# One step of a two-layer hybrid decoder: p and gate weights fetched and split early, 1/rms by Ln and Exp, the beginning in another order

## What is computed

```python
for l in range(2):
    h = h + 0.5 * swiglu(rms_norm(h, g1[l]), wi1[l], wo1[l])      # ffn 2l
    h = h + mixer[l](rms_norm(h, gm[l]))                          # conv and mLSTM, or two attentions
    h = h + 0.5 * swiglu(rms_norm(h, g2[l]), wi2[l], wo2[l])      # ffn 2l+1
    h = h + sigmoid(rms_norm(h, gp[l]) @ wg[l]) * (p[l] @ wp[l])  # the gate phase, "ple"
y = rms_norm(h, g_final)

def rms_norm(x, g, eps=1e-6):
    return x * lax.rsqrt(jnp.mean(x * x, axis=-1, keepdims=True) + eps) * g
```

## Time and profile before

| | us |
|---|---|
| median of 3 runs | 2738.8 |
| lowest and highest | 2735.88 and 2739.21 |
| the profiled execution, as a run | 2746.85 |
| its span, from the first to the last instruction | 2745.0 |
| PE busy in it | 2599.5 |

### The profile page before, as it was taken

The page is one execution under the profiler, slowest core; times in us unless marked ns, Lnnn a source line. Parts: engine busy times, 40 slices in busy tenths (PEclk is TensorE's granted clock), DMA queues, the critical chain, the costliest instruction groups (busy, mean ns, idle before and its releaser), DMA issues. The chain is left out here.

```text
span 2745.0 us, 44639 instructions
## 1 busy us (share of the span) xinstructions
PE 2599.5 (95%) x18322; PEld 2456.3 (89%) x18322; DVE 927.2 (34%) x1558; ACT 767.5 (28%) x954; POOL 811.0 (30%) x206
## 2 busy tenths in 40 slices
PE   7999999898889999999999999999789799999997
PEld 6999999895579999999999999999455599999997
DVE  4211224686653211224321122311755432202234
ACT  4222223223223222224322222311444432212232
POOL 3333333221023333333333343432000033343332
PEclk9999999998789999999999999999876699999998
DMA  4222223310112222222222222234211022222122
GB/s 145 82 83 90 77 77 110 70 62 31 48 60 82 76 81 88 80 72 76 102 76 77 100 77 77 101 112 157 93 62 47 16 77 77 76 92 77 69 85 73
DMA packets 66902, 220.57 MB, mean 80 GB/s; under 512 B 14007, under 2 KB 31287, under 8 KB 51195
## 3 DMA queue, kind: packets, MB, share of 16 engines
q1 hardware_dynamic: 51280, 200.68, 21.2%
q10 hardware_dynamic: 15530, 18.63, 2.4%
HBM read 207.95 MB, written 11.33 MB: 80 GB/s over the span
## 5 line engine op out<-in xcount | busy, mean ns | idle before, releaser
L430 POOL TENSOR_TENSOR wl<-raw,wr 128x2048 fp32r<-128x2048 f32 (+2 forms) x200 | 807.3, 4036 | 1905.9 <-ACT wr L858 1905.9
L440 PE MATMUL ps<-xr,wr 128*128 128x256 f32 (+1 forms) x2432 | 727.3, 299 | 39.5 <-POOL wl L430 23.4
L442 PE MATMUL ps<-xr,wl 128*128 128x256 f32 (+1 forms) x2432 | 724.9, 298 | 0.0
L441 PE MATMUL ps<-xl,wr 128*128 128x256 f32 (+1 forms) x2432 | 724.9, 298 | 0.0
L440 PEld LDWEIGHTS ps<-xr,wr 128*128 128x128 f32 x2432 | 466.2, 192 | 43.5 <-issue 36.2
L440 PE MATMUL ps<-x2r,wr 128*128 128x256 f32 (+1 forms) x1664 | 491.8, 296 | 0.5 <-POOL wl L430 0.5
L442 PE MATMUL ps<-x2r,wl 128*128 128x256 f32 (+1 forms) x1664 | 490.0, 294 | 0.0
L441 PE MATMUL ps<-x2l,wr 128*128 128x256 f32 (+1 forms) x1664 | 489.9, 294 | 0.0
L441 PEld LDWEIGHTS ps<-xl,wr 128*128 128x128 f32 x2432 | 466.2, 192 | 0.2
L442 PEld LDWEIGHTS ps<-xr,wl 128*128 128x128 f32 x2432 | 465.7, 191 | 0.0
L858 ACT ACTIVATE wr<-raw 128x2048 fp32r<-128x2048 f32 (+1 forms) x200 | 351.6, 1758 | 369.6 <-PE ps L442 294.3
(11 more groups left out here) (312 smaller groups left out, 2027.8 us busy)
## 6 DMA issues: line engine op xcount, KB each, us to landing
raw<-in_up SPq DMA_DIRECT2D x88, 1024.0 KB, 4.8
raw<-in_down SPq DMA_DIRECT2D x32, 768.0 KB, 4.2
raw<-in_mixin SPq DMA_DIRECT2D x24, 1024.0 KB, 4.8
raw<-in_down SPq DMA_DIRECT2D x32, 640.0 KB, 3.9
raw<-in_ple SPq DMA_DIRECT2D x16, 640.0 KB, 3.9
raw<-in_mixout SPq DMA_DIRECT2D x8, 1024.0 KB, 4.9
kc<-in_kc SPq DMA_DIRECT2D x32, 256.0 KB, 3.5
vc<-in_vc SPq DMA_DIRECT2D x32, 256.0 KB, 3.5
```

Of the source, the lines that this page charges most:

```text
L430: e.tensor_tensor(wl[s][:, 0:p.width], raw[s][:, 0:p.width], wr[s][:, 0:p.width].bitcast(F32), ALU.subtract).then_inc(S(f"w_split{s}"), 1)
L440: e.matmul(out, wrt, xrt, start=first, stop=False)
L441: e.matmul(out, wrt, xlt, start=False, stop=False)
L442: return e.matmul(out, wlt, xrt, start=False, stop=last)
```

## The change

- **p.** `praw` moves to memory behind x2l, and its rounded part and residual take the last two blocks of `hr` and `hl`, which the second chunk of an ffn doesn't use. The load is issued ahead of ffn 1 and ffn 3; ACT rounds it and DVE makes its residual between "up" and "down" of the second chunk of these ffn.
- **Gate weights and history.** The gate weights are loaded at the beginning, and rounded and split in ffn 0, between "up" and "down" of the first chunk. The history is loaded from SP's queue once the last "down" tile of ffn 0 is done. ACT stores the fourth bias row in "glu" behind the first Sigmoid, and DVE waits for the stores in the first block of "glu", where it also sets the fringe of `vn`.
- **1/rms.** `root` makes Ln and then Exp of -0.5 times it on ACT, with the table set for both loaded ahead of its wait; the reciprocal on DVE goes.
- **The beginning.** POOL no longer sets `raw` to zero. The first weight load comes right behind the parameters on SP's queue, then four of the eight blocks of x (the odd ones), then, once block 4 has landed, the second weight load. ACT issues the even blocks, loads the table set ahead, and rounds the first weights behind the second block's square. Squares go to `sq` and `hd` in turn and are summed in two PSUM banks, the last sum into `acc`; the residual of the third block comes behind the first three sums. The first norm's `norm_sum` stands in the second tile's third step.

The diff, with the unchanged lines around it cut:

```diff
     x2l = sb("x2l", [P, KD, T], F32R, at=[X2_AT + KD * T * 4])
-    praw = sb("praw", [P, KP, T], at=z)
-    pr = sb("pr", [P, KP, T], F32R, at=z)
-    pl = sb("pl", [P, KP, T], F32R, at=z)
+    praw = sb("praw", [P, KP, T], at=[X2_AT + 2 * KD * T * 4])
+    assert CHUNKS[0] - CHUNKS[1] == KP
+    pr, pl = hr[:, CHUNKS[1]:, :], hl[:, CHUNKS[1]:, :]
     z = [ZONE]
...
         e.dma_start(prm[:], A["prm"]).then_inc(S("prm_loaded"), 16)
-        def load_pair(p, i):
+        def load_pair(p, i, first=False):
             for s in range(2):
+                if first and s == 1:
+                    for j in range(1, KD, 2):
+                        e.dma_start(h[:, j, :], A["xT"][:, j, :]).then_inc(S(f"h_loaded{j}"), 16)
+                    e.wait_ge(S(f"h_loaded{KD // 2}"), 16)
...
             p = ph[name]
+            if name in (order[0], "glu"):
+                load_pair(p, 0, first=name != "glu")
+            if name == "glu":
+                e.wait_ge(S("tile_done"), done_at(("down", 0, 1), KD - 1))
+                e.dma_start(us[:, :, :, 0:HIST], A["hist"]).then_inc(S("hist_loaded"), 16)
             if name != ("out", 1):
-                with e.Fori(0, p.nb // 2) as i:
+                with e.Fori(1 if name in (order[0], "glu") else 0, p.nb // 2) as i:
                     load_pair(p, i)
...
         for s in range(2):
-            e.memset(raw[s][:], 0.0).then_inc(S(f"w_split{s}"), 1)
+            e.nop().then_inc(S(f"w_split{s}"), 1)
         for name in order:
...
             p = ph[name]
+            norm_at = (0, 5) if norm else (1, 2)
...
                         for k in range(kn_):
-                            if first and t == 0 and k == 5:
+                            if first and (t, k) == norm_at:
                                 norm_sum(norm)
...
+            e.preload_act_table_set("natural_log_exp_and_others")
             e.wait_ge(S("ss_ready"), m + 1)
-            e.activation(two(R[:]), psn, ACT.Sqrt, scale=1.0 / D, bias=eps6[:, 0:1]).then_inc(S("root_ready"), 1)
+            e.activation(two(R[:]), psn, ACT.Ln, scale=1.0 / D, bias=eps6[:, 0:1]).then_inc(S("root_ready"), 1)
+            e.wait_ge(S("root_ready"), m + 1)
+            e.activation(R[:], R[:], ACT.Exp, scale=-0.5).then_inc(S("R_ready"), 1)
...
                     store_bias_row(2 * c)
+                    if c == 0:
+                        e.wait_ge(S("wg_loaded"), 16)
+                        e.activation(wgr[:], wgraw[:], ACT.Copy).then_inc(S("wgr_ready"), 1)
+                if n % 2 and c == 1:
+                    e.wait_ge(S("p_loaded"), 16 * (n // 2 + 1))
+                    e.activation(pr, praw[:], ACT.Copy).then_inc(S("pr_ready"), 1)
                 down_phase(n, c, m + 1 if c else None)
-                if n == 0:
-                    store_bias_row(2 * c + 1)
-
-
-        for j in range(KD):
+                if (n, c) == (0, 0):
+                    store_bias_row(1)
+
+
+        for j in range(0, KD, 2):
             e.dma_start(h[:, j, :], A["xT"][:, j, :]).then_inc(S(f"h_loaded{j}"), 16)
+        e.preload_act_table_set("natural_log_exp_and_others")
         e.wait_ge(S("prm_loaded"), 16)
...
             head(0, j, (S(f"h_loaded{j}"), 16))
-            square(0, j, None)
-            if j == KD // 2:
+            if j >= 2:
+                e.wait_ge(S("acc_done"), j - 1)
+            e.activation((sq, hd)[j % 2][:], h[:, j, :], ACT.Square).then_inc(S("sq_ready"), 1)
+            if j == 1:
                 round_block(order[0], 0, 0, first=True)
...
         e.dma_start(pages[:], A["pages"]).then_inc(S("pages_loaded"), 16)
+        e.dma_start(wgraw[:], A["wg"]).then_inc(S("wg_loaded"), 16)
         e.wait_ge(S("ones_ready"), 3)
...
-        e.dma_start(wgraw[:], A["wg"]).then_inc(S("wg_loaded"), 16)
-        e.dma_start(us[:, :, :, 0:HIST], A["hist"]).then_inc(S("hist_loaded"), 16)
-        e.wait_ge(S("wg_loaded"), 16)
-        e.activation(wgr[:], wgraw[:], ACT.Copy).then_inc(S("wgr_ready"), 1)
         for n in blocks("glu", 1):
...
             e.activation(sg[:], tu[:], ACT.Sigmoid).then_inc(S("glu_sig"), 1)
+            if n == 0:
+                store_bias_row(3)
...
         e.wait_ge(S("m_stored"), 16)
+        e.dma_start(praw[:], A["pT"][0]).then_inc(S("p_loaded"), 16)
         ffn(1, 2)
...
             m = 4 * l + 4
-            e.dma_start(praw[:], A["pT"][l]).then_inc(S("p_loaded"), 16)
             name = ("ple", l)
             for n in blocks(name, m - 1):
-                if n == 0:
-                    e.wait_ge(S("p_loaded"), 16 * (l + 1))
-                    e.activation(pr[:], praw[:], ACT.Copy).then_inc(S("pr_ready"), 1)
                 e.wait_ge(S("tile_evacuated"), evac_at(name, 2 * n))
...
         e.wait_ge(S("kv_stored"), 32)
+        e.dma_start(praw[:], A["pT"][1]).then_inc(S("p_loaded"), 16)
         ffn(3, 6)
...
         def factor(m):
-            e.wait_ge(S("root_ready"), m + 1)
-            e.reciprocal(R[:], R[:]).then_inc(S("R_ready"), 1)
             e.wait_ge(S("R_ready"), m + 1)
...
                     copy_bias_row(2 * c)
+                    if c == 0:
+                        e.wait_ge(S("wgr_ready"), 1)
+                        e.tensor_tensor(wgl[:], wgraw[:], wgr[:].bitcast(F32), ALU.subtract).then_inc(S("wg_split"), 2)
+                if n % 2 and c == 1:
+                    e.wait_ge(S("pr_ready"), n // 2 + 1)
+                    e.tensor_tensor(pl, praw[:], pr.bitcast(F32), ALU.subtract).then_inc(S("p_split"), 1)
                 if c:
...
+        acc_ps = ps[:, 6:8, 0:HALF]
         e.wait_ge(S("prm_loaded"), 16)
...
             e.wait_ge(S(f"h_loaded{j}"), 16)
-            rest(0, j)
-            add_square(0, j, j == 0)
+            if j != 2:
+                rest(0, j)
+            for q in {1: (0, 1, 2), 2: ()}.get(j, (j,) if j else ()):
+                e.wait_ge(S("sq_ready"), q + 1)
+                src = two((sq, hd)[q % 2][:])
+                if q == 0:
+                    e.tensor_copy(acc_ps, src).then_inc(S("acc_done"), 1)
+                else:
+                    e.wait_ge(S("acc_done"), q)
+                    e.tensor_tensor(two(acc[:]) if q == KD - 1 else acc_ps, acc_ps, src, ALU.add
+                                    ).then_inc(S("acc_done"), 1)
+            if j == 1:
+                e.wait_ge(S("h_loaded2"), 16)
+                rest(0, 2)
         factor(0)
...
-        e.wait_ge(S("grep_stored"), 16 * HEADS)
         e.wait_ge(S("cst_loaded"), 16)
         step(e.memset(up[:, :, 0:HIST], 0.0))
-        e.memset(vn[:, :, :, P:P + 1], 1.0).then_inc(S("vn_ones"), 1)
-        e.wait_ge(S("wgr_ready"), 1)
-        e.tensor_tensor(wgl[:], wgraw[:], wgr[:].bitcast(F32), ALU.subtract).then_inc(S("wg_split"), 2)
...
             if j == 0:
+                e.wait_ge(S("grep_stored"), 16 * HEADS)
+                e.memset(vn[:, :, :, P:P + 1], 1.0).then_inc(S("vn_ones"), 1)
                 e.wait_ge(S("hist_loaded"), 16)
...
             name, m = ("ple", l), 4 * l + 4
-            e.wait_ge(S("pr_ready"), l + 1)
-            e.tensor_tensor(pl[:], praw[:], pr[:].bitcast(F32), ALU.subtract).then_inc(S("p_split"), 1)
             zero_acc(m)
```

## The result

The changed kernel took 2713.07 us (median of four executions, 2701.79 to 2715.04), the kernel before 2738.41 beside it. The ratio is 0.9895, 95% interval 0.9882 to 0.9907, which is 28.7 us less (25.5 to 32.3) and puts the changed kernel at 2709.7 on the scale of the kernel before. The two medians by themselves are 25.3 us apart. The sign and the parts were forecast, the size was not: 19.2 us were forecast, and 2709.7 lies just under the range's lower end, 2711, which the interval (2706.1 to 2712.9) still takes in.

A forecast was written before the change was run, and what follows sets the result against it. TensorE, busy 95% of the span, was taken as the bound, so only its waits counted. 3.1 + 2.2 + 12.3 - 0.2 + 1.8 = 19.2 us off the median gave 2719.6 us, range 2711 to 2728.

The forecast's parts named there:

- toss: Row chain before the first key tile: 0.1 us decides whether splits hold additions, 8.0 us; changed loses 0.14, only it wins 0.08.
- 1/rms at the end: End of program: Ln and Exp replace root and reciprocal ahead of the output scaling, 3.1 us gained.
- The gate phases with the last down phases: Waits on p's residual and lower clock go, 12.3 us gained; later GpSimd splits in ffn 1 and 3 lose 0.2.
- what is late next: First gate phase, once p's wait is gone: R comes next, with a margin of 0.8 us, so no wait.
- Glu: Entry of glu: R comes 8.4 us sooner where 2.2 are needed, so 2.2 us gained.
- TensorE itself is then next: Entry of glu: with R early, TensorE's own work sets the pace, so only the 2.2 us wait is gained.
- the vn memset: Glu's first block: rival that a 4.65 us split holds the memset, 2.5 more with lower clock, 2726.7; chance 0.04.
- The beginning: Program start: first weight split 2.6 us sooner, 0.8 given back, 1.8 us gained (3.6 gained to 1.0 lost).
- the 0.8 us that were to go back: Program start: x's last residual done at 25.8, while TensorE asks for it at 25.0.
- the other five roots: Five other places computing 1/rms: TensorE has a tile to run meanwhile, so faster R gains nothing, apart from p.
- The rival by which the beginning gives nothing: Program start: x's second block comes with the last bytes, plus 1.8 to 2.8 us, 2722; chance 0.12.
- The attention stage: Rival from 1920 to 2180 us: clock mixture of 0.73 falls worse; with 30 us changing over, 2749.6; chance 0.04.

The follow-up runs named there:

- The run without the toss: Kernel before with the row chain's two gate-bias additions reading PSUM, so that no weight split can hold them: 2736.48 us, ratio 0.9992.
- the two pairs: Traces of the kernel before and the changed kernel, as they were and both with row chain through PSUM and idle attention matmuls: spans 45.1 and 24.4 us apart.
- without the two chances: Row chain through PSUM and idle attention matmuls added to both kernels: kernel before 2714.34 us, changed kernel 2688.97 us.

## Why the prediction was right or wrong

**The base was right.** The sum was taken off the median and not off the profiled execution, since the profiled one looked like a lost toss. The run without the toss bears that out for most executions of the kernel before.

**1/rms at the end, 3.1 forecast:** 3.1. **The gate phases with the last down phases, 12.3 less 0.2 forecast:** 12.0 and 12.1 in the two pairs (5.7, and 6.3 to 6.4), with the lower clock behind the wait counted as the earlier trace rows had it; even the 0.26 us wait on GpSimd came at the second block. That they need both p and 1/rms is what "what is late next" had found: R with a margin of 0.8. The loss of 0.2 in both last down phases together is 0.18 in each, 0.36 in both: that of ffn 1 and that of ffn 3 take 63.65 us in the traces with p early and 63.47 in the others.

**Glu, 2.2 forecast: 3.7 to 4.0.** The step that failed is "TensorE itself is then next". The wait was priced by its length alone, although the same argument two paragraphs on took the lower clock behind a wait into the sum. The windows above show 0.50 and 0.75 behind it. How much comes back is itself a draw of the kernel before: from the first down phase to the key phase its glu entry takes 333.1 to 334.8 us in the five traces that have it unedited, the changed kernel's 330.6 in all seven, so the part is worth 2.4 to 4.1. The fourth bias row's store and the vn memset took nothing back. The memset came 0.3 us ahead of the split that it was feared to meet, so it doesn't test that rival; a memset of 128x576 inside another split took 0.54 us, as outside one.

**The beginning, 1.8 forecast: 3.1** in the mean of the traces, 2.5 and 3.3 in the two pairs. Two terms were mis-sized. The split came at 12.75, not 13.3. And the residuals and sums behind it follow each other at 0.70 us, not 0.8 (from 19.22 to 23.40 are six steps), so the last residual is done at 24.2 and not at 25.8, ahead of TensorE: the 0.8 us that were to go back did not. One thing the forecast didn't see: it said of the other five roots that a faster R is worth nothing there, and with the beginning reordered it saves a wait of 0.91 us at the first, as the run of the beginning alone shows. The rival by which the beginning gives nothing did not come about: the order in which things arrive was worth more than 3 us at the first matmul. The rule that the Trainium skill (DMA: Bandwidth & Descriptors, section "Issuing engines are not separate DMA queues") states, that loads issued from several engines share the same 16 DMA engines, agrees with the trace: from 4 to 10 us the loads moved 382 to 449 GB/s, 390 to 433 in the kernel before.

**The toss.** The mechanism was right, its place in the argument wrong. It was treated as one outcome for each kernel; it falls anew in each execution of the same kernel, and a median of four holds what those four happened to get.

**The attention stage.** This is where the range failed. The rival had the right place and the right cause, a mixture of two levels that may fall otherwise, and only its unlucky side was priced, at 0.04. The step that failed is that the lucky side got neither a price nor a chance, and no reason for that; three runs within 3.4 us, named against the rival, were too few to rule it out. That side, 10 to 14 us less, is shown by two of ten traces, and 8 of 71 later executions of the kernel before have a granted clock of 0.955 or more. By their granted clock two of the four first timed executions had it (0.962 and 0.960 over the span, 0.952 and 0.953 the other two), none of the four of the kernel before beside them seems to (2735.88 at the least).

So of the 28.7 us, 21.6 are steps of the change, 2.4 of these more than forecast, some 3 are open, and the rest goes, as far as the granted clocks tell, to four executions that were luckier than most: the same kernel measured again was 21.6 us faster, and without the two chances it is 25.4.

## What to carry to other kernels

Price a wait of TensorE as its length and the lower clock behind it, and read that from the windows behind the wait, each time. Where a trace has stretches at both levels, or an operation that a split catches by a tenth of a microsecond, take two traces of the same kernel before believing a difference, and give both signs room in the range. And such a chance can be taken out: an operand left in PSUM, and a few idle matmuls in a known wait, were worth 25 us here, as much as the whole change.

## What the runs showed of the hardware that was not expected

More matmuls made the kernel faster. Forty-eight idle ones (each counts twice in the trace), about 12 us of TensorE's time, took the attention stage from 268.0 or 255.6 us to 246.5, with the granted clock over the stage at 0.85 instead of 0.74 or 0.82:

```profile
1892.10:2138.65 246.55, 206.14 (x1186) 0.85 0.20 65
```

The waits that were followed by the lower level are short: 2.14 us here, 2.2 at glu, 1.84 in a gate phase. And the same wait need not be followed by it: behind 2.19 us at glu the clock was at 0.50, behind 2.22 us in another kernel at 1.00. The issue time of the same four DMAs on ScalarE varied from 2.65 to 3.6 us (the first three take 0.6 each, the last 0.7 to 1.6), which decided over 8 us elsewhere.
